# Later start of a window-row copy, another order of filler products, and a decode step cut into halves and quarters

## What is computed

```python
def _compress(kv, pe, w1, b1, w2):
    ...
    blk = jnp.swapaxes(blk, 2, 3).reshape(B, n_cmp, h, CMP_BLOCK * d)
    return jax.nn.silu(blk @ w1 + b1) @ w2
...
    s = jnp.einsum('btkgd,bckd->btkgc', qg, ck) * scale              # compressed branch
    p = jnp.where(cvalid, jax.nn.softmax(jnp.where(cvalid, s, NEG), axis=-1), 0.0)
    o_cmp = jnp.einsum('btkgc,bckd->btkgd', p, cv.astype(jnp.float32))
...
    gates = jax.nn.sigmoid(jnp.stack([ma, mb, mc], axis=2))          # ma, mb, mc: part of h @ w_in
    m = jnp.sum(gates * jnp.einsum('blnc,ncd->blnd', ys, w_branch), axis=2)
    y = x + m @ w_out
    return y, rows, wfull[:, -min(WINDOW, lw):], s_new.astype(dt)    # the third: 511 old rows and 1 new
```

## Time and profile before

| what | before |
|---|---|
| median of 3 runs | 970.44 us (968.86 to 975.02) |
| the profiled execution | 968.84 us |
| its span, first to last instruction | 967.2 us |
| mean granted TensorE clock | 0.995 |
| PE busy | 933.7 us, 97% of the span |
| DVE, ACT, POOL busy | 50%, 31%, 14% |
| DMA moved | 188.98 MB, mean 195 GB/s |

### The profile page before, as it was taken

One profiled execution on the slowest core, in us unless ns is written; L12 is line 12 of the kernel. 1 busy time (PEld: TensorE's weight loads), 2 busy tenths in 40 slices (PEclk: granted clock), 3 DMA queues, 4 the chain that ended last, 5 costly groups with the idle time before them and its releaser, 6 DMA issues.

```text
span 967.2 us, 17080 instructions
## 1 busy us (share of the span) xinstructions
PE 933.7 (97%) x6250; PEld 752.9 (78%) x6250; DVE 485.2 (50%) x1374; ACT 304.5 (31%) x659; POOL 132.5 (14%) x258
## 2 busy tenths in 40 slices
PE   9999989999999999899999999899999999998998
PEld 7888768777677777788888887687777767877887
DVE  4123547877753676024250335488686436751331
ACT  2235432246633113300111363322476331233000
POOL 0420000002032261000060000000020413600000
PEclk9999999999999999999999999999999999999999
DMA  7554555344189698333544436462341996972432
GB/s 281 189 169 159 183 204 219 130 143 175 44 298 383 237 386 291 105 131 131 167 163 170 142 142 212 168 249 98 142 175 44 335 389 250 385 244 93 170 132 88
DMA packets 56501, 188.98 MB, mean 195 GB/s; under 512 B 9186, under 2 KB 22882, under 8 KB 43874
## 3 DMA queue, kind: packets, MB, share of 16 engines
q1 hardware_dynamic: 43138, 138.56, 41.0%
q0 software_dynamic: 12992, 49.16, 13.4%
q10 hardware_dynamic: 288, 0.18, 0.1%
HBM read 177.47 MB, written 18.77 MB: 203 GB/s over the span
## 4 chain that ended last, share of the span: by engine, by line
PE 78%; DVE 8%; issue 5%; DVEq 4%; ACT 3%; DMA 2%; ACTq 0%; SPq 0%
PE ps L868 20%; PE ps L995 18%; PE ps L1341 9%; PE ps L1234 4%; PE ps L1354 3%; PE ps L1348 3%; DVE arena L1883 2%; DMA arena<-in_win_k_dram 2%; PE ps L1145 2%; PE ps L1133 2%; PE ps L893 2%; PE ps L857 1%; PE ps L1312 1%; PE ps L1113 1%; DVE arena L1985 1%
## 5 line engine op out<-in xcount | busy, mean ns | idle before, releaser
L868 PE MATMUL ps<-hT,slab 128*128 128x264 f32 (+1 forms) x1184 | 271.6, 388 | 0.0
L868 PEld LDWEIGHTS ps<-hT,slab 128*128 128x128 f32 (+1 forms) x1184 | 222.5, 190 | 39.0 <-issue 1.1
L995 PE MATMUL ps<-hT,slab 128*128 128x264 f32 x768 | 181.1, 392 | 4.2 <-issue 2.5
L995 PEld LDWEIGHTS ps<-hT,slab 128*128 128x128 f32 x768 | 144.5, 192 | 35.2 <-issue 4.9
L1366 ACT ACTIVATE arena<-ps 128x512 f32<-128x512 f32 (+21 forms) x152 | 69.8, 485 | 183.9 <-PE ps L868 66.7
L1341 PE MATMUL ps<-Y,slab 128*128 128x264 f32 x384 | 85.8, 386 | 0.0
L1341 PEld LDWEIGHTS ps<-Y,slab 128*128 128x128 f32 x384 | 73.0, 190 | 12.5
L1760 DVE SCALAR_TENSOR_TENSOR arena<-arena,small 128x264 f32<-128x264 f32 x26 | 11.0, 489 | 110.1 <-ACT arena L1441 110.1
L1234 PEld LDWEIGHTS ps<-arena,w 128*128 128x128 f32 x512 | 58.4, 192 | 10.0 <-issue 6.6
L1234 PE MATMUL ps<-arena,w 128*128 128x128 f32 x512 | 61.4, 278 | 0.0
L593 POOL DMA_DIRECT2D arena<-in_pages_kv_dram x64 | 33.3, 520 | 159.4 <-DVEq L2271 121.6
(11 more groups left out here) (365 smaller groups left out, 1205.8 us busy)
## 6 DMA issues: line engine op xcount, KB each, us to landing
slab<-in_weights_dram SPq DMA_DIRECT2D x86, 1024.0 KB, 5.0
arena<-in_pages_kv_dram SPq DMA_DIRECT2D x64, 256.0 KB, 8.5
arena<-in_pages_kv_dram POOLq DMA_DIRECT2D x64, 256.0 KB, 6.6
arena<-in_pages_kv_dram POOLq DMA_DIRECT2D x64, 128.0 KB, 7.4
arena<-in_pages_kv_dram SPq DMA_DIRECT2D x64, 128.0 KB, 11.3
out_dram<-in_state_win_dram POOLq DMA_DIRECT2D x2, 4088.0 KB, 24.3
arena<-in_state_hgrn_dram SPq DMA_DIRECT2D x2, 2048.0 KB, 10.6
out_dram<-arena POOLq DMA_DIRECT2D x2, 2048.0 KB, 7.1
```

Source lines behind the costliest of these rows:

```text
L868: last = mm(ps[0:job[3], n % 2, 0:LT], v[:, k, job[2]:job[2] + job[3]], hT[:, k, :], start=(k == 0), stop=(k == KD - 1))
L995: last = mm(ps[:, bank, 0:LT], v[:, k, (d % 2) * 128:(d % 2) * 128 + 128], hT[:, k, :], start=(k == 0), stop=(k == KD - 1))
```

## The change

Six edits; line numbers of before.

1. POOL's copy of the window rows waits for the index keys of pair 3 instead of "dot 2".
2. Prompt attention: the order of the two mixes after each value step, and of the numbers waited for, is changed (`mix(0)` ahead of `mix(6)`).
3. Stage cp: the 16 compression products are put between the 8 products of a mix, two behind each; the mixes that follow stand elsewhere (one ahead of `s` instead of behind it) and in other banks, and the mix behind `gb 0` waits for ACT's `ev` alone.
4. `s cmp` uses stationary blocks of 32 columns in two column quarters of the array; the values of the compressed branch use 8 stationary columns for each sequence directly from `PTc`; `PTcx`, its clearing and its copy are gone, and its results lie in `so` as a fourth part.
5. The value products run k = 1 first, and a mix follows each group; the mix behind "oT" is gone.
6. The spilled gates go to another place (`at(24576, ...)`), and SP issues their reload when PE has marked "PT".

```diff
-        PTcx = w1_flat[0:NCS, 0:NS * (ROWS + NH)]
...
-        sig = ((at(0, KD * LT),), (at(RAW1, KD * LT),), (at(RAW1 - LT, LT), in_w1))
+        sig = ((at(24576, KD * LT),), (at(RAW1, KD * LT),), (at(RAW1 - LT, LT), in_w1))
...
-        dx_p = Steps("dx_p", [f"x {k}" for k in range(2)])
+        dx_p = Steps("dx_p", ["x 1", "x 0"])
...
                 sp.wait_ge(spill_out, l * 16 + 16)
-                sp.wait_ge(dx_p.sem, dx_p(l, "x 0"))
+                sp.wait_ge(dc_p.sem, dc_p(l, "PT"))
                 sp.dma_start(sig[0][0], spill).then_inc(back_in, 16)
...
-                pool.wait_ge(pidx_p.sem, pidx_p(l, "dot 2"))
+                for i in range(2):
+                    pool.wait_ge(ik_in[3][i], (l + 1) * NPG * 16)
                 pool.dma_start(s_win[l1].rearrange("a s w c -> (a s) w c"),
                                state_win[l1, :, 1:WIN, :].rearrange("a s w c -> (a s) w c")).then_inc(win_out, 16)
...
                     if a < 2:
+                        pe.wait_ge(at_v.sem, at_v(l, f"s {a + 1}01"))
+                        mix(0)
                         pe.wait_ge(at_v.sem, at_v(l, f"ev {a}0"))
                         mix(6)
-                        pe.wait_ge(at_v.sem, at_v(l, f"s {a + 1}01"))
-                        mix(0)
...
-                for kv in range(2):
-                    for t in range(ST):
+                n = next(mixes)
+                v = arrived(f"m{n // KD}{n % KD // 2}")
+                for k in range(KD):
+                    turn = mm(ps[:, 2, 0:LT], v[:, k, (n % 2) * 128:(n % 2) * 128 + 128], hT[:, k, :], start=(k == 0), stop=(k == KD - 1))
+                    for i in (2 * k, 2 * k + 1):
+                        kv, t = i // ST, i % ST
                         last = mm(ps[:, kv, 0:36], w1[:, kv, t, :], XP[:, kv, t, :], start=(t == 0), stop=(t == ST - 1))
                 last.then_inc(cp_p.sem, cp_p.mark("h"))
-                mix(2)
+                turn.then_inc(mx_p.sem, mx_p.mark(f"m {n}"))
+                mix(3)
...
-                for b in range(NS):
-                    last = mm(ps[0:ROWS, 3, 0:NCS], QC[:, 1, b * ROWS:(b + 1) * ROWS], ckd[:, b, :], start=(b == 0), stop=(b == NS - 1))
+                for p in range(NPAIR):
+                    for e in range(2):
+                        last = mm(ps[quarter[e], 3, 0:NCS], queries_of(1, p + NPAIR * e), ckd[:, p + NPAIR * e, :], start=(p == 0), stop=(p == NPAIR - 1))
...
-                pe.wait_ge(dc_v.sem, dc_v(l, "ptx cmp"))
                 for b in range(NS):
-                    mm(ps[0:ROWS, 7, 0:128], PTcx[:, b * ROWS:(b + 1) * ROWS], CV[0:NCS, b, :], start=(b == 0), stop=(b == NS - 1))
+                    mm(ps[eight[b % 4], 7, b // 4 * 128:b // 4 * 128 + 128], PTc[0:NCS, b * NH:(b + 1) * NH], CV[0:NCS, b, :], start=True, stop=True)
...
-                for k in range(2):
+                for k in (1, 0):
...
                     last.then_inc(dx_p.sem, dx_p.mark(f"x {k}"))
-                mix(3, after=21)
+                    mix(3, after=22 - k)
                 pe.wait_ge(dc_v.sem, dc_v(l, "scaled"))
                 for k in range(2):
-                    for a in range(3):
-                        nc.tensor.transpose(ps[:, 6 + k, a * 128:a * 128 + 96 + NH], so[all4, k, a * 128:a * 128 + 128], ident[all4, all4])
-                last = nc.tensor.transpose(ps[:, 6, 384:384 + ROWS], soc, ident[0:ROWS, 0:ROWS])
+                    for a in range(4):
+                        last = nc.tensor.transpose(ps[:, 6 + k, a * 128:a * 128 + 96 + NH], so[all4, k, a * 128:a * 128 + 128], ident[all4, all4])
...
-                mix(5)
```

More of the change, by code:

```diff
@@ L436, in hybrid_step @@
         raw0 = at(5280, KD * LT)
[L437 to L438 removed]
+        sig = ((at(24576, KD * LT),), (at(RAW1, KD * LT),), (at(RAW1 - LT, LT), in_w1))
+        sig_at = [at(24576 + LT * d, LT) for d in range(KD)] + mix_at[KD:]
         mT = at(6336, KD, LT)
@@ L1164, in _ @@
                 mm(ps[0:NCP, 5, 0:128], hidP[:, 1, 0:NCP], w2[:, 1, :], start=True, stop=True).then_inc(cp_p.sem, cp_p.mark("out"))
-                mix(3)
+                mix(2, after=8)
                 pe.wait_ge(cp_a.sem, cp_a(l, "out"))
@@ L1171, in _ @@
                 last.then_inc(cp_p.sem, cp_p.mark("s"))
-                mix(2, after=8)
                 mix(3, after=9)
-                mix(2, after=10)
-                mixed(12)
+                pe.wait_ge(cp_v.sem, cp_v(l, "s"))
+                mix(4)
+                mixed(11)
                 pe.wait_ge(cp_v.sem, cp_v(l, "n"))
@@ L1199, in _ @@
                     if c == 0:
+                        pe.wait_ge(cp_a.sem, cp_a(l, "ev"))
+                        mix(7)
+                    elif c == 1:
                         pe.wait_ge(cp_v.sem, cp_v(l, "ev"))
-                        pe.wait_ge(cp_a.sem, cp_a(l, "ev"))
-                    if c < 2:
-                        mix(6 + c)
+                        mix(6)
                     else:
-                        mix(6, after=14)
+                        mix(7, after=14)
                 def page_scores(u):
@@ L1556, in exps @@
                         if a and t:
-                            take((6, 0)[g])
+                            take((0, 6)[g])
                 exps(0)
@@ L1597, in _ @@
                 take(3)
-                take(2)
+                take(4)
                 act.wait_ge(cp_p.sem, cp_p(l, "t"))
@@ L1607, in _ @@
                 for c in range(3):
-                    take((6, 7, 6)[c])
+                    take((7, 6, 7)[c])
                 def pair_blocks(p, rows):
@@ L1668, in _ @@
                 take(3)
+                take(3, ACT.Sigmoid)
                 act.drain()
@@ L1676, in _ @@
                 take(3, ACT.Sigmoid)
-                take(5, ACT.Sigmoid)
         @block.vector
@@ L2146, in _ @@
                 join(3)
-                ve.memset(PTcx, 0.0)
                 ve.wait_ge(dc_a.sem, dc_a(l, "scores"))
```

38 lines of the change are left out of this document (16 added, 22 removed).

## The result

| | before | after |
|---|---|---|
| median | 969.9 us | 946.65 us |
| lowest to highest | 968.86 to 975.02 (4 runs) | 946.1 to 948.4 (4 runs) |
| the profiled execution | 968.84 | 946.56 |
| its span | 967.2 | 944.9 |
| its mean granted clock | 0.995 | 0.998 |

The ratio is 0.9752, 95% interval 0.9721 to 0.9783. One run among all that follow, of shift_blocks_before, took 1213 us at a mean clock of 0.749 and is left out everywhere. The forecast was 949.5 us, a ratio of 0.978, with a range of 943.5 to 958.

A forecast was written before the change was run, and what follows sets the result against it. TensorE, busy 933.7 of 967.2 us, was taken as the bound. Terms, with +0.1 for one more transpose, summed to -19.6 from 968.84, giving 949.2; 0.3 added for the median made 949.5 us, range 943.5 to 958.

The forecast's parts named there:

- Copy, -9.5: Index keys at L949: with the window-row copy later, 5.9 us of waits and 3.6 us of clock dips go.
- Attention, -2.3: Prompt attention: the new mix order removes four waits of 0.57 us at L1133, 2.3 us.
- Compression between a mix's products, -0.2: Stage cp: weight loads behind short passes stay exposed, so interleaving gives only 0.2 us for both layers.
- rival 4: Compression: weight loads run further ahead, so interleaving gives 1.9 us a layer, total 945.3 us; chance 0.08.
- Softmax, -1.0: Mixes around the softmax: it still ends before two covering mixes, and the 1.0 us wait at L1179 goes.
- `gb` and page scores, -0.8: Waits behind `gb` and at the page scores (L1213): 0.4 us saved at each.
- Quarters, -2.9: Decode's `s cmp` and compressed values: column quarters and 8 stationary columns save 0.4 and 1.05 us a layer.
- Halves and reload, -3.0: Decode values: instruction-fetch waits behind loads, with dips, fall from 7.0 to 4.0 us; 2.9 us wait remains in layer 0.
- Rival 1: Slab g00 is held by the copy instead of the keys; the gates wait 2.3 us a layer, 956.5 us; chance 0.13.

The follow-up runs named there:

- shift_blocks_before: The kernel before without the five warm-up products (20 instructions) at TensorE's start: 966.3 us, ratio to before 0.9964.
- copy_back: The changed kernel with POOL's copy of the window rows waiting for "dot 2" again, as before: 955.6 us, ratio to before 0.9844.
- attention_order_back: The changed kernel with the old order of the two mixes in the prompt attention: 952.1 us, ratio to before 0.9812.
- compression_apart: The changed kernel with the 16 compression products in front of a plain mix again: 951.3 us, ratio to before 0.9817.

## Why the prediction was right, point by point

- **Copy, -9.5.** The mechanism was right: the keys' packets took turns with packets of 64 KB, and so the last of them came with the copy's end. Waits and dips came to 9.3 in the pair of profiles and 9.0 by taking the edit back; by the runs of the edit alone 7.4. "I take the upper end because the dip shows only behind such waits" was the weak step: dips also stand behind waits of 0.6 us and behind none, and a wait of 2.8 us in copy_back had none; of eight such waits in four profiles four had one. With their mean wait of 5.5 us, the lost overlap and half the dips the term is some 7.5 us.
- **Attention, -2.3.** Right in its place, too small: 3.0 by the timelines, 3.2 by attention_order_back, since a removed wait gives back 0.17 us of overlap besides its row. The other 0.35 us of that stage is the wait at L1033, which was in no term.
- **Compression between a mix's products, -0.2.** For the work it was so: 0 to 0.1 us a layer by the timelines. The price of weight loads was right and rival 4 is out. (The 7.4 to 7.5 us forecast for the compression with its mix were the busy times added up; from start to start it is 7.15.) What may be missing is the dip behind the 16 products in a row, which the profile of before did not have; see compression_apart.
- **Softmax, -1.0.** 1.3 together with the compression's 0.2, and no wait at `t`. The mechanism shows on DVE: its idle time ahead of the reduction is 0.47 us in after, 3.48 before. No run takes this part back.
- **`gb` and page scores, -0.8.** 0.5 and 1.6. The wait for window keys in layer 0, which I expected to stay, did not show in after; in other profiles it is 0.3 to 1.8 us, in one layer or the other, so this part is a matter of the execution. In return came 0.8 us at L1247. The dips behind `gb 0` were in no term: the profile of after has none, its variants have 14 in 16 layers (see the end), at 1.7 us each.
- **Quarters, -2.9.** 3.2: 0.64 us for the scores where I took 0.7, 0.62 for the values where I took 0.46, and more than 1.5 before.
- **Halves and reload, -3.0.** 4.9, by the mechanism stated, and at the place stated: the wait of 2.36 us at the end of the first value group of layer 0, none in layer 1. The 0.8 us for a dip behind it and the 0.3 for layer 1 did not come, and the wait is 0.5 smaller than the 2.9. I had also left out the lost overlap and a wait of 0.35 in the kernel before. No run takes the halves or the earlier reload back; the runs on the fetch bear out the wait, not the size of the whole part.
- **Rival 1** was ruled out by more than I thought: g00 lands in 4.9 us, by 127.5, and it is issued 1.2 us before the copy (122.64 against 123.88). "8 x 2.5 us" assumed that both start together. (Its time is 956.8 by its own terms, not 956.5, and rival 4's 945.6, not 945.3; nothing hangs on either.)
- The terms together gave 19.6 us where the profiles show 22.3: they were 4.4 us too small, most of it in the halves (2.0), the page scores (1.2) and the attention stage (1.1), and the dip at `s cmp` of layer 0, which was in no term and belongs to the execution, takes 1.7 back. So the forecast of 949.5 came out 2.9 us above the measured 946.65, near partly because of that dip.

## What to carry to other kernels

A big copy that nobody waits for is not free: small transfers on the same engines get one packet through for each of its packets, and land with its end. Here a later start cured it, and so did pieces of 16 KB, with which the copy also ended 8 us sooner. An "issue" wait beside a burst of loads may be the fetch of instructions; add or remove a few instructions and see whether it moves with the count. And where runs carry a mean clock, split the time into full-clock time and the rest before believing a difference of 1%.

## What was not expected of the hardware

- A dip of the granted clock costs 1.66 us a time (a mix of 3.83 takes 5.49) and comes in some executions and not in others at the same place. Behind `gb 0` the mix waited 0.64 us in the nine profiles of the changed family and had a dip in 14 of 18 layers; it waited 0.86 in the five of the other family and had one in 2 of 10. So the length of the wait alone does not decide it, and what does stays open. Runs of the kernel before differ mostly by dips, from 0.998 (963.8 us) to 0.983 (979.0).
- 16 products of 36 columns in a row were followed by a dip in 3 of 6 profiles (3 of 12 layers), although TensorE had not been idle just before; two short products behind each long one, never in 8. The numbers are small, and no cause is shown.
- A fetch of 16 KB of instructions was late by up to 2.8 us behind loads of 1 to 2 MB, in both kernels, and the wait moved with the count of instructions.
- A DRAM-to-DRAM copy of 4 MB took 24.3 us in pieces of 64 KB and 16.5 in pieces of 16 KB, which also ran on more engines. Beside it, one small packet of the other queue ran for each of its packets.
